# Attention in steps of two heads, with values stationary on the two halves of TensorE's columns

## What is computed

```python
s = jnp.einsum('bqhd,bqkhd->bhqk', qb, kg).astype(jnp.float32) * scale
s = jnp.where(valid[:, None], s, -jnp.inf)
p = jax.nn.softmax(s, axis=-1).astype(vg.dtype)
return jnp.einsum('bhqk,bqkhd->bqhd', p, vg)
...
return jnp.concatenate([a_out, b_out], axis=-1) @ w_out
```

## Time and profile before

| | us |
|---|---|
| median of three runs (2996.25 to 2997.68) | 2997.05 |
| the profiled execution, its own time | 3001.99 |
| its span, first to last instruction | 3000.4 |
| TensorE busy (97%) | 2903.0 |
| VectorE busy (51%) | 1543.2 |
| ScalarE busy (28%) | 847.9 |
| stage of layer 0, from its first product to that of `pe_mixed_out` | 581.05 to 647.92 |
| stage of layer 1, likewise | 1574.02 to 1640.87 |
| stage of the third block, likewise | 2541.19 to 2602.23 |

### The profile page before, as it was taken

One profiled execution on the slowest core, in us unless ns is written; L12 is line 12 of the kernel. 1 busy time (PEld: TensorE's weight loads), 2 busy tenths in 40 slices (PEclk: granted clock), 3 DMA queues, 4 the chain that ended last, 5 costly groups with the idle time before them and its releaser, 6 DMA issues.

```text
span 3000.4 us, 35621 instructions
## 1 busy us (share of the span) xinstructions
PE 2903.0 (97%) x13730; PEld 2402.4 (80%) x13730; DVE 1543.2 (51%) x2213; ACT 847.9 (28%) x954; POOL 256.7 (9%) x111
## 2 busy tenths in 40 slices
PE   4999989999999999999999999999999999999999
PEld 3888878778888888887778788888888878878887
DVE  6654646856623465355595654355433456544232
ACT  3221233333212232122323321243212245432121
POOL 1000005510000000000361000000000013100000
PEclk9999999999999999999999999999999999999999
DMA  5543523124622245253221452332222221122222
GB/s 224 196 168 131 191 104 98 63 74 144 223 78 103 94 163 201 98 203 138 79 69 43 153 211 98 112 121 77 102 101 84 102 88 43 57 95 108 79 100 81
DMA packets 61626, 352.25 MB, mean 117 GB/s; under 512 B 7634, under 2 KB 8018, under 8 KB 34004
## 3 DMA queue, kind: packets, MB, share of 16 engines
q1 hardware_dynamic: 60436, 348.95, 32.5%
q10 hardware_dynamic: 1088, 1.97, 0.4%
HBM read 346.83 MB, written 2.10 MB: 116 GB/s over the span
## 4 chain that ended last, share of the span: by engine, by line
PE 88%; DVE 6%; DVEq 2%; ACT 1%; issue 1%; POOL 0%; DMA 0%; SPq 0%; ACTq 0%; POOLq 0%
PE bank L300 28%; PE bank L301 27%; PE bank L302 27%; DVE m_m L1357 2%; PE bank L976 2%; DVEq L1356 2%; PE bank L308 1%; PE bank L966 1%; ACT m_wH L277 1%; PE bank L295 0%; DVE m_masks L1361 0%; DVE m_wL L270 0%; DVE m_hL L429 0%; DVE m_guL L1092 0%; POOL m_wL L255 0%
## 5 line engine op out<-in xcount | busy, mean ns | idle before, releaser
L300 PE MATMUL bank<-m_hH,m_wH 128*128 128x512 f32 x2464 | 968.3, 393 | 14.5 <-DVE m_hL L429 11.2
L301 PE MATMUL bank<-m_hL,m_wH 128*128 128x512 f32 x2464 | 961.6, 390 | 0.0
L302 PE MATMUL bank<-m_hH,m_wL 128*128 128x512 f32 x2464 | 961.5, 390 | 0.0
L270 DVE TENSOR_TENSOR m_wL<-m_wraw,m_wH 128x2048 fp32r<-128x2048 f32 (+2 forms) x186 | 464.3, 2496 | 590.1 <-ACT m_wH L277 590.1
L277 ACT ACTIVATE m_wH<-m_wraw 128x2048 fp32r<-128x2048 f32 (+3 forms) x238 | 465.2, 1955 | 906.2 <-PE bank L302 905.1
L300 PEld LDWEIGHTS bank<-m_hH,m_wH 128*128 128x128 f32 x2464 | 464.1, 188 | 117.6 <-issue 19.9
L302 PEld LDWEIGHTS bank<-m_hH,m_wL 128*128 128x128 f32 x2464 | 464.2, 188 | 97.6
L301 PEld LDWEIGHTS bank<-m_hL,m_wH 128*128 128x128 f32 x2464 | 464.3, 188 | 94.1 <-issue 0.2
L300 PE MATMUL bank<-m_guH,m_wH 128*128 128x512 f32 x1248 | 494.4, 396 | 1.5 <-DVE m_guL L1092 1.5
L302 PE MATMUL bank<-m_guH,m_wL 128*128 128x512 f32 x1248 | 487.3, 390 | 0.0
L301 PE MATMUL bank<-m_guL,m_wH 128*128 128x512 f32 x1248 | 487.2, 390 | 0.0
(11 more groups left out here) (261 smaller groups left out, 2114.7 us busy)
## 6 DMA issues: line engine op xcount, KB each, us to landing
m_wraw<-in_ffn_in SPq DMA_DIRECT2D x132, 1024.0 KB, 4.9
m_mod_w<-in_ada_w SPq DMA_DIRECT2D x144, 512.0 KB, 4.4
m_wraw<-in_ffn_out_a SPq DMA_DIRECT2D x24, 1536.0 KB, 8.0
m_wraw<-in_mix SPq DMA_DIRECT2D x32, 1024.0 KB, 4.8
m_wraw<-in_ffn_out_b SPq DMA_DIRECT2D x24, 1280.0 KB, 5.8
m_wraw<-in_mix SPq DMA_DIRECT2D x24, 512.0 KB, 3.6
m_mod_big<-in_ada_w SPq DMA_DIRECT2D x4, 2048.0 KB, 17.6
m_x<-in_x SPq DMA_DIRECT2D x1, 2048.0 KB, 9.4
```

The source lines that it names most:

```text
L270: nc.vector.tensor_tensor(m.wL[:, j, 0:size], m.wraw[:, j, 0:size], f(m.wH[:, j, 0:size]), ALU.subtract).then_inc(s.low, 1)
L300: nc.tensor.matmul(out, a[0], b[0], start=first, stop=False)
L301: nc.tensor.matmul(out, a[0], b[1], start=False, stop=False)
L302: return nc.tensor.matmul(out, a[1], b[0], start=False, stop=last)
```

## The change

The stage goes in 16 steps j of two heads, with four buffers in place of three for `m.sm`, `m.p` and `m.pT`.

- `product(j)`: the values are stationary (64 columns) and the transposed probabilities move (128 columns). The even head's output goes to partitions 0 to 63, the odd head's to 64 to 127, so the two use the two halves of TensorE's columns. The result lies as the projection needs it; `out` is gone.
- The sums now lie across the wrong axis. `inverse` (VectorE) takes the reciprocals of a block, `spread(i)` (TensorE) makes eight fp32 products of a broadcast column with the identity into bank 7, `inverse` (ScalarE) copies them to `m.rs`, and `normalize` multiplies by it. `high` and `low` read `m.bn`.
- The groups' tiles all use bank 6, so that the first group of a tile waits for the `update` of the tile before it. `WOVEN` gives the groups of each step.
- The order within a step on TensorE: scores(j), groups, turn(j-1), spread of a block that is complete, product(j-2).

The diff, cut to its core:

```diff
@@ -136,10 +136,11 @@
     m.sq2 = at("sq2", 32 * K, [2, T])
     m.acc2 = at("acc2", 36 * K, [T])
 
-    m.sm = at("sm", 16 * K, [3, T])
-    m.p = at("p", 22 * K, [3, T])
-    m.pT = at("pT", 28 * K, [3, T])
-    m.bn = at("bn", 34 * K, [2, T])
+    m.sm = at("sm", 16 * K, [4, T])
+    m.p = at("p", 24 * K, [4, T])
+    m.pT = at("pT", 32 * K, [4, T])
+    m.rs = at("rs", 40 * K, [T])
+    m.bn = at("bn", 42 * K, [2, T])
...
-    N = TT * HEADS
-    EXTRA = {0: 2, 1: 2, 32: 1, 33: 1, 34: 1, 35: 2, 36: 2}
...
+    N = TT * HEADS // 2
+    PAIRS = HEADS // 2
+    WOVEN = (4, 1, 1, 2, 2, 2, 2, 1, 1, 1, 1, 2, 2, 2, 2, 2, 2, 2)
...
+
+    def tiles_done(self, j):
+
+        return range(self.groups[j] // 4, self.groups[j + 1] // 4) if 0 <= j < self.N + 2 else ()
...
+    def last(self, j):
+
+        return j // self.PAIRS if 0 <= j < self.N and j % self.PAIRS == self.PAIRS - 1 else None
...
+        def spread(i):
+
+            pe.wait_ge(s.rv, i + 1)
+            if i >= 1:
+                pe.wait_ge(s.rsc, i)
+            for h in range(HEADS):
+                mm = nc.tensor.matmul(m.bank[7][HD * (h % 2):HD * (h % 2 + 1), h // 2 * P:(h // 2 + 1) * P],
+                                      m.rinv[:, i * HEADS + h:i * HEADS + h + 1].to_broadcast([P, HD]), m.ident,
+                                      start=True, stop=True)
+            mm.then_inc(s.rsp, 1)
+
+        def product(j):
+            i, d = j // self.PAIRS, j % self.PAIRS
+            tiles = self.of(2 * j)[4]
+            if d == 0 and i >= 2:
+                pe.wait_ge(s.on, i - 1)
+            pe.wait_ge(s.pc, 2 * j + 2)
             for b in range(tiles):
...
-        def product(n):
...
-            for b in range(tiles):
-                mm = nc.tensor.matmul(m.bank[i % 2][:, h * HD:(h + 1) * HD], m.pT[:, n % 3, b * P:(b + 1) * P],
-                                      self.value(h, b), start=(b == 0), stop=(b == tiles - 1))
+                for e in range(2):
+                    n = 2 * j + e
+                    mm = nc.tensor.matmul(m.bank[i % 2][HD * e:HD * (e + 1), d * P:(d + 1) * P], self.value(n % HEADS, b),
+                                          m.pT[:, n % 4, b * P:(b + 1) * P], start=(b == 0), stop=(b == tiles - 1))
             mm.then_inc(s.av, 1)
-
-        def out(n):
...
-                i = n // HEADS
-                pe.wait_ge(s.on, i + 1)
-                for d in range(4):
-                    mm = nc.tensor.transpose(m.bank[i % 2][:, d * P:(d + 1) * P], m.bn[:, i % 2, d * P:(d + 1) * P], m.ident)
-                mm.then_inc(s.bt, 1)
-        for n in range(self.N + 5):
...
+        for j in range(self.N + 2):
+            if j < self.N:
+                scores(j)
+            for g in range(self.groups[j], self.groups[j + 1]):
+                if j < self.N + 1:
+                    self.pe_group(pe, nc, m, s, g)
+            if 1 <= j <= self.N:
+                turn(j - 1)
+            if self.last(j - 1) is not None:
+                spread(self.last(j - 1))
+            if j >= 2:
+                product(j - 2)
+        for g in range(self.groups[self.N + 1], self.groups[self.N + 2]):
+            self.pe_group(pe, nc, m, s, g)
 
...
-        if k == 0 and d >= 2:
-            pe.wait_ge(s.y, 4 + self.y0 + d - 1)
+        if k == 0 and d >= 1:
+            pe.wait_ge(s.y, 4 + self.y0 + d)
         w = m.wH[:, slot, at:at + P], m.wL[:, slot, at:at + P]
-        mm = pe_3(nc, m.bank[6 + d % 2][:], w, (m.guH[:, k], m.guL[:, k]), k == 0, k == 3)
+        mm = pe_3(nc, m.bank[6][:], w, (m.guH[:, k], m.guL[:, k]), k == 0, k == 3)
         if k == 3:
             mm.then_inc(s.mm, 1)
...
-                nc.vector.reciprocal(r, m.sums[:, i * HEADS:(i + 1) * HEADS])
-                dve.drain()
...
-                nc.vector.tensor_tensor(m.bn[:, i % 2].rearrange("p (h e) -> p h e", h=HEADS),
-                                        m.bank[i % 2][:].rearrange("p (h e) -> p h e", h=HEADS),
-                                        r.unsqueeze(2).to_broadcast([P, HEADS, HD]), ALU.mult).then_inc(s.on, 1)
...
+        def inverse(i):
+            at = slice(i * HEADS, (i + 1) * HEADS)
+            dve.wait_ge(s.ex, HEADS * (i + 1))
+            nc.vector.reciprocal(m.rinv[:, at], m.sums[:, at]).then_inc(s.rv, 1)
+
+        def normalize(i):
+            dve.wait_ge(s.av, self.PAIRS * (i + 1))
+            dve.wait_ge(s.rsc, i + 1)
+            nc.vector.tensor_tensor(m.bn[:, i % 2], m.bank[i % 2][:], m.rs[:], ALU.mult).then_inc(s.on, 1)
+
+        def low(i):
+            dve.wait_ge(s.ch, i + 1)
+            nc.vector.tensor_tensor(m.guL[:, 4:8, i * P:(i + 1) * P], m.bn[:, i % 2].rearrange("p (d t) -> p d t", d=4),
+                                    f(m.guH[:, 4:8, i * P:(i + 1) * P]), ALU.subtract).then_inc(s.cl, 1)
...
+        for j in range(self.N + 3):
+            if j < self.N:
+                mask(2 * j)
+                mask(2 * j + 1)
+            if self.last(j - 1) is not None:
+                inverse(self.last(j - 1))
+            if 1 <= j <= self.N:
+                copy(2 * j - 2)
+                copy(2 * j - 1)
+            for d in self.tiles_done(j):
                 update(d)
+            if self.last(j - 2) is not None:
+                normalize(self.last(j - 2))
+            if self.last(j - 3) is not None:
+                low(self.last(j - 3))
...
+        def inverse(i):
+            act.wait_ge(s.rsp, i + 1)
+            if i >= 1:
+                act.wait_ge(s.on, i)
+            nc.scalar.activation(m.rs[:], m.bank[7][:], ACT.Copy).then_inc(s.rsc, 1)
+
+        def high(i):
+            act.wait_ge(s.on, i + 1)
+            nc.scalar.activation(m.guH[:, 4:8, i * P:(i + 1) * P], m.bn[:, i % 2].rearrange("p (d t) -> p d t", d=4),
+                                 ACT.Copy).then_inc(s.ch, 1)
+        for j in range(self.N + 3):
+            if j < self.N:
+                exponential(2 * j)
+                exponential(2 * j + 1)
+            if self.last(j - 1) is not None:
+                inverse(self.last(j - 1))
...
+            for d in self.tiles_done(j):
                 if d % 2:
                     act_next(act, nc, m, s, self.u + d // 2, HALF)
+            if self.last(j - 3) is not None:
+                high(self.last(j - 3))
```

More of the change, by code:

```diff
@@ L926, in __init__ @@
         self.groups = [0]
-        for n in range(self.N + 5):
-            here = self.EXTRA.get(n, n % 2 if n < HEADS else int(n % 4 != 1))
+        for here in self.WOVEN:
             self.groups.append(self.groups[-1] + here)
[L930 to L940, removed]
+        assert self.groups[-1] == 4 * KD and len(self.WOVEN) == self.N + 2
+    def tiles_done(self, j):
+        return range(self.groups[j] // 4, self.groups[j + 1] // 4) if 0 <= j < self.N + 2 else ()
     def of(self, n):
@@ L944, in of, with scores @@
         return q, k, mask, tiles * P, tiles, scale
+    def last(self, j):
+        return j // self.PAIRS if 0 <= j < self.N and j % self.PAIRS == self.PAIRS - 1 else None
     def pe(self, pe, nc, m, s):
[L947 to L954, removed]
+        def scores(j):
+            if j >= 1:
+                pe.wait_ge(s.sm, 2 * j)
+            if j < self.PAIRS:
+                pe.wait_ge(s.parts, self.parts(2 * j))
+            two = [(m.bank[4 + e][:, 0:self.of(2 * j + e)[3]],) + self.of(2 * j + e)[:2] for e in range(2)]
@@ L987, in pe @@
[L987 to L990, removed]
+            for e in range(2):
+                n = 2 * j + e
+                pe.wait_ge(s.ex, n + 1)
+                if j >= 1:
+                    pe.wait_ge(s.pc, n - 1)
+                for b in range(self.of(n)[4]):
+                    mm = nc.tensor.transpose(m.bank[2 + e][:, b * P:(b + 1) * P], m.p[:, n % 4, b * P:(b + 1) * P], m.ident)
+                mm.then_inc(s.tr, 1)
@@ new lines, in spread @@
+        def spread(i):
[13 more added lines that the diff above has]
+            pe.wait_ge(s.pc, 2 * j + 2)
+            for b in range(tiles):
+                for e in range(2):
+                    n = 2 * j + e
+                    mm = nc.tensor.matmul(m.bank[i % 2][HD * e:HD * (e + 1), d * P:(d + 1) * P], self.value(n % HEADS, b),
+                                          m.pT[:, n % 4, b * P:(b + 1) * P], start=(b == 0), stop=(b == tiles - 1))
+            mm.then_inc(s.av, 1)
@@ L1009, in mask @@
             dve.wait_ge(s.sc, n + 1)
[L1010 to L1013 removed]
+            if n >= 4:
+                dve.wait_ge(s.ex, n - 3)
+            nc.vector.tensor_tensor_reduce(out=m.sm[:, n % 4, 0:w], in0=m.bank[4 + n % 2][:, 0:w], in1=mask,
                                            scale=-scale * HD ** -0.5, scalar=BIG, op0=ALU.add, op1=ALU.min,
@@ L1044, in update @@
         def update(d):
             dve.wait_ge(s.mm, 4 + 2 * self.u + d + 1)
-            nc.vector.scalar_tensor_tensor(out=m.x[:, d], in0=m.bank[6 + d % 2][:], scalar=gate(d), in1=m.x[:, d],
```

(10 more changed lines are left out.)

52 lines of the change are left out of this document (9 added, 43 removed).

## The result

The changed kernel takes 3008.23 us (median of 8 runs) against 2996.98 us of the kernel before beside it: ratio 1.0036, interval [1.0025, 1.0047], **slower by 0.36%**, 11.3 us. That is inside the range, on the side that had the largest chance, and 6 us above the predicted number. The profiled execution took 3009.89 us, its span is 3008.3.

A forecast was written before the change was run, and what follows sets the result against it. TensorE, busy 97% of the span, was taken as the bound. Terms -22.3 - 4.3 + 10.6 + 6.6 + 1.5 + 8.4 + 4.8 = +5.3 us gave 3007.3, or 3002 us as median; range 2988 to 3018.

The forecast's parts named there:

- Term 1: Value products: both heads run side by side on column halves, 0.22 us for both heads and a tile; -22.3 us together.
- serial rival: Value products and spreads: column halves do not run side by side, +36 us, giving 3038 us; chance 13%.
- the one of partial overlap: Value products and spreads: column halves overlap in part, 0.30 us for both heads and a tile, +13, 3015 us; chance 14%.
- Term 2: Transposes behind the value products go: 0.36 us, four times a stage; -4.3 us.
- Term 3: Spreads come: eight fp32 products on alternating halves, 0.88 us, four times a stage; +10.6 us.
- Term 4: Changes of shape on TensorE, 0.20 us assumed into the columns' shape; +6.6 us for three stages.
- Term 5: Waits inside a stage: copy waits go, first groups of tiles wait for update instead; +1.5 us.
- One of my signs of being wrong: Blocks 1 to 3: VectorE or ScalarE hold TensorE up by more than 0.3 us a step.
- Term 6: End of the stage: TensorE idles 3.0 us behind the chain update, normalize, high, low; +2.8 a stage, +8.4 us.
- Term 7: Behind the stage's 3.0 us pause the clock drops to 1.2 GHz for 3.4 us: 1.6 us a stage, +4.8 us.
- A stage of layer 0 from 66.9 us to about 68.5: Layer 0: a stage was to lengthen from 66.9 us to about 68.5.
- another such sign: Outside the three stages: a difference showing there would mean the prediction was wrong.

The follow-up runs named there:

- experiment 4: The change with a head pair's value products issued head by head instead of tile by tile; 3015.99 us, 0.23% above the change.
- experiment 7: The change with each of a tile's spread products issued twice, writing the same values; 3020.72 us, 0.38% above the change.
- experiment 1: The change with a stage's last update moved behind low on VectorE and the last weight conversion behind the last high on ScalarE; 2995.69 us.
- Experiment 2: The change with only the conversion of the next weight unit moved behind the last high on ScalarE; 3007.16 us.
- experiments 2, 3 and 4: Of these, 3 is the change with 14 unread products put behind each stage's last groups to fill the pause; 3007.83 us.

## Why the prediction was right, and where it was off

The direction and the range came out, and the stages' arithmetic closes. Windows of the change, layer 0 and third block, each up to the end of the pause and from there to the norm:

```profile
581.38:649.50 68.12, 61.59 (x496) 0.97 0.14 45
649.50:677.38 27.88, 24.71 (x96) 0.90 0.33 113
2545.45:2608.49 63.04, 57.37 (x474) 0.99 0.10 35
2608.49:2636.38 27.89, 24.84 (x97) 0.89 0.33 111
```

The same two windows before, layer 0:

```profile
581.05:647.92 66.87, 65.64 (x449) 0.97 0.13 45
647.92:673.15 25.23, 22.06 (x96) 1.00 0.36 124
```

The first part grew by 1.25 us. My terms 1 to 6 for such a stage are -7.7 - 1.4 + 3.5 + 2.2 + 0.6 + 2.8 = 0.0; with `low` 1.35 longer that is the number measured, within 0.1. The clock comes on top, behind the pause: 27.88 - 25.23 = 2.65.

- **Term 1, value products:** right. 0.22 us for both heads and a tile. The serial rival and the one of partial overlap fall with these rows, and experiment 4 shows what losing the alternation costs. The rule that stationary loads overlap only where row groups differ (the Trainium skill, TensorE: Matmul & The Clock Gate, Part 3) does not hold for these column halves: all rows are shared, and 16 rows with a load each start 0.055 us apart.
- **Term 2, transposes behind:** gone, -4.3, as the list of work has it; not run alone.
- **Term 3, spreads:** right: 0.88 said, 0.93 by the row, 0.87 by experiment 7.
- **Term 4, changes of shape:** somewhat too high. Into the columns' shape: 632.37 - 631.41 = 0.96 for eight turns that need 0.87, so 0.09. Out of it, the next scores start at 633.40, 1.03 behind; less 16 rows (0.88) and the 0.10 that scores paid before, 0.05. Together 0.14 where I took 0.20, 1.0 us a stage less. Spreads were 0.05 longer each, 0.2 a stage. So the list lacks 0.8 us a stage, 2.4 in all, which this term hid: that the sum closes is in part luck. Half of it is in the waits of term 5.
- **Term 5, waits inside:** said 0.4, 0.2, 0.3 and 0.66. Measured in layer 0:

```profile
588.13 0.50 PE L301 MATMUL bank<-m_guH,m_wH 128*128 128x512 f32 x1 [0.36 <-DVE m_x L1057]
594.76 0.47 PE L301 MATMUL bank<-m_guH,m_wH 128*128 128x512 f32 x1 [0.31 <-DVE m_x L1057]
601.71 0.50 PE L301 MATMUL bank<-m_guH,m_wH 128*128 128x512 f32 x1 [0.37 <-DVE m_x L1057]
638.43 0.50 PE L301 MATMUL bank<-m_guH,m_wH 128*128 128x512 f32 x1 [0.58 <-DVE m_x L1057]
```

  The idle time shown starts at a product's end. From start to start, against a step without a wait, they cost 0.44, 0.38, 0.44 and 0.71 us: 2.0, where the term says 1.6. The other 0.4 of the 0.8 I did not find. One of my signs of being wrong has come, that VectorE holds TensorE up by more than 0.3 us in a step of blocks 1 to 3: the last three of these waits are longer. That sign contradicted term 5, which had 0.66 for the last.

- **Term 6, the end of the stage:** the mechanism was right, `normalize` queued behind an `update` that it doesn't need; **the size was off in one link**. "`low` (0.69)" came from a row in which `low` read one operand from PSUM. In the change both operands lie in SBUF, and ScalarE hands GpSimd its weights 0.9 us before, so it took 2.04 to 2.10 at the end of each stage: idle 4.35, not 3.0, 1.35 x 3 = **+4.1 us**. The Trainium skill (SBUF — State Buffer, "SBUF: two separate sides") says that a VectorE instruction with two SBUF inputs and a GpSimd instruction that reads SBUF lock each other out of a shared pair of ports for the whole instruction. The rows agree: `low` ended 0.55 us after GpSimd's 648.89. The trace of before had it already. Over its whole program, the same subtraction with both inputs in SBUF (L1092), and `normalize` with one input from PSUM (L1033), min/median/max in ns:

```profile
L1092 DVE TENSOR_TENSOR m_guL<-m_ra,m_guH x8: 691/1158/1627, 572.2 to 1574.6; 128x512 fp32r<-128x512 f32 x8
```

```profile
L1033 DVE TENSOR_TENSOR m_bn<-bank,m_rinv x12: 691/692/693, 597.6 to 2598.6; 128x512 f32<-128x512 f32 x12
```

  The four of L1092 that ran beside GpSimd took 1.62 us, the four without it 0.69. Three of L1033 lay wholly beside GpSimd, and in the change six of L1048, and took no longer than the others. I had not asked which operands had moved out of PSUM.
- **Term 7, the clock:** right in kind, a pause over 3 us and 0.50 behind it; 2.65 measured a stage, 1.6 said, **+3.2 us** for three. The half clock held for longer than my one row of 3.4 us: products 0.43 apart from 649.50 to 654.8 in this execution. But the cost behind one and the same pause varies: in the nine stages with a pause of 4.18 us (the change, experiments 4 and 7) the stretch to the norm was 1.4 to 2.8 us longer than in experiment 1, and 1.4 to 1.6 in three of them. So 1.6 was within what such a pause costs, and too low for this execution. In experiment 2 a pause of 2.83 cost 1.6 us in layer 0 (26.83 against 25.22), and in the third block one of 2.77 cost nothing, so near there it can go either way.
- **Sum:** 5.3 + 4.1 + 3.2 = 12.6 for the stages, 12.5 measured. In the medians it is 11.3, and the two mis-sized terms, 7.3 us, cover the 6 that the predicted 3002 lacks.
- "A stage of layer 0 from 66.9 us to about 68.5": 68.1 came, by luck. Up to the pause's end my terms make 66.9; the 1.6 for the clock, which I had added, falls behind that point, and what came in its place is `low`.
- A difference outside the three stages was another such sign: one shows, 4.6 us in the profiled pair, but it is no work of the change: the execution of the kernel before lost 38.0 us of clock there, the other 31.3. It swings by 10 us between kernels that share that code.

## What to carry to other kernels

When an edit moves an operand from PSUM to SBUF, price the instruction again with its neighbour on GpSimd in view, and look who hands GpSimd its work just then. At the end of a stage, order each queue so that nothing stands ahead of the instructions that the next stage waits for, and keep enough independent TensorE work behind the last product to cover that chain: here these two edits, which take away no work, turned 0.36% slower into 0.38% faster. And cut the span at stages before reading a total: 10 us of scatter in code that didn't change hid effects of 5.

## What the runs showed of the hardware that was not expected

- A VectorE `tensor_tensor` of 128 x 512 with both inputs in SBUF took 1.62 to 2.10 us beside GpSimd in the rows shown (the stages' last `low`, and L1092), 0.69 without it; with one input in PSUM it took 0.68 or 0.69 either way.
- Products on two column halves need not alternate one by one: two tiles a head (eight rows) took 0.66 us in either order, three 0.88 or 1.14, four 1.09 or 1.58.
- Behind the same pause of 4.18 us the half clock cost between 1.4 and 2.8 us, in nine stages.
- Half clock comes and goes between executions in code that no edit touched: the granted clock at one norm was 0.72 in experiments 2, 3 and 4 and 1.00 in the change, and outside the stages 25.5 to 38.0 us of clock were lost in an execution.
